# Trunk kernel on one Trainium2 core: the end of each layer of the second trunk with tokens in the partitions

## The reference

```
def trunk_layer(x, ctx, c, c_ctx, p, ang_r, ang_c, need_ctx):
    shift, scale, gate = jnp.split(jax.nn.silu(c) @ p['w_ada'] + p['b_ada'], 3, axis=-1)
    shift_c, scale_c, gate_c = jnp.split(jax.nn.silu(c_ctx) @ p['w_ada'] + p['b_ada'], 3, axis=-1)
    h = x * (1.0 + scale[:, None, :]) + shift[:, None, :]
    hc = ctx * (1.0 + scale_c) + shift_c
    ...                                   # 16 projections of h and hc, three branches
    out = merge(y_attn, y_gla, y_sgu, m_a, m_g, m_s)          # m @ p['w_out'] at its end
    x_new = layer_norm(DEEPNORM_ALPHA * x + gate[:, None, :] * out, p['post_g'], p['post_b'])
    if not need_ctx:
        return x_new, ctx                 # layer 1: only the 512 latent tokens
    ...
    ctx_new = layer_norm(DEEPNORM_ALPHA * ctx + gate_c * out_c, p['post_g'], p['post_b'])
    return x_new, ctx_new
```

## Time and profile before

| | us |
|---|---|
| median of 3 runs | 3522.41 (3520.08 to 3523.33) |
| the profiled execution | 3518.86 |
| its span in the trace | 3516.7 |
| PE busy in the span | 3188.0 |
| DVE busy | 1906.8 |
| ACT busy | 1178.4 |
| POOL busy | 208.4 |

### The profile page before, as it was taken

The page is one execution under the profiler, slowest core; times in us unless marked ns, Lnnn a source line. Parts: engine busy times, 40 slices in busy tenths (PEclk is TensorE's granted clock), DMA queues, the critical chain, the costliest instruction groups (busy, mean ns, idle before and its releaser), DMA issues.

```text
span 3516.7 us, 43743 instructions
## 1 busy us (share of the span) xinstructions
PE 3188.0 (91%) x18216; PEld 2645.0 (75%) x18216; DVE 1906.8 (54%) x2789; ACT 1178.4 (34%) x1763; POOL 208.4 (6%) x144
## 2 busy tenths in 40 slices
PE   7997889999988889999898999988998888997997
PEld 6886778888877667777777878756887777775776
DVE  7756555665434755777454443574434544457543
ACT  4234341221232544222342333253221534425322
POOL 0003100000010000000002120000001012100001
PEclk9999999999989999999899999999999799999997
DMA  5543123333211003555221123102113112320221
GB/s 203 178 154 126 55 78 126 121 131 120 84 55 60 1 13 121 179 176 177 88 86 69 65 75 110 42 1 81 54 66 96 71 66 88 103 81 7 97 94 58
DMA packets 91373, 321.84 MB, mean 92 GB/s; under 512 B 10070, under 2 KB 11991, under 8 KB 90025
## 3 DMA queue, kind: packets, MB, share of 16 engines
q1 hardware_dynamic: 81236, 289.43, 24.4%
q10 hardware_dynamic: 9940, 29.61, 2.3%
HBM read 297.26 MB, written 21.74 MB: 91 GB/s over the span
## 4 chain that ended last, share of the span: by engine, by line
PE 77%; DVE 10%; ACT 8%; issue 4%; DMA 1%; ACTq 0%; POOL 0%; SPq 0%; POOLq 0%; DVEq 0%
PE PS L384 76%; ACT whi L195 2%; ACT Pq L1274 1%; DVE STs L1311 1%; PE PS L387 1%; ACT nt L611 1%; DVE JUNK L514 1%; DVE stage L514 1%; DVE STq L1311 1%; DVE wlo L209 1%; ACT Ps L1274 1%; DMA Ht<-in_hT 1%; ACT U L616 0%; DVE fg L721 0%; ACT Ht L2304 0%
## 5 line engine op out<-in xcount | busy, mean ns | idle before, releaser
L384 PE MATMUL PS<-U,whi 128*128 128x512 f32 (+1 forms) x5408 | 1178.0, 363 | 93.7 <-DVE U L641 27.9
L384 PEld LDWEIGHTS PS<-U,whi 128*128 128x128 f32 x5408 | 913.8, 193 | 283.2 <-issue 59.3
L209 DVE TENSOR_TENSOR wlo<-stage,whi 128x1024 fp32r<-128x1024 f32 x339 | 417.0, 1232 | 1060.7 <-ACT whi L195 1060.1
L195 ACT ACTIVATE whi<-stage 128x1024 fp32r<-128x1024 f32 x339 | 358.3, 1058 | 1425.7 <-PE PS L384 1403.5
L384 PE MATMUL PS<-U,wlo 128*128 128x512 f32 (+1 forms) x2704 | 620.9, 355 | 0.0
L384 PE MATMUL PS<-Y,whi 128*128 128x512 f32 (+1 forms) x2240 | 582.9, 364 | 18.9 <-DVE Y L723 12.9
L384 PEld LDWEIGHTS PS<-U,wlo 128*128 128x128 f32 x2704 | 458.1, 189 | 79.7
L384 PEld LDWEIGHTS PS<-Y,whi 128*128 128x128 f32 x2240 | 397.3, 191 | 93.8 <-DVE Y L723 14.8
L384 PE MATMUL PS<-Y,wlo 128*128 128x512 f32 (+1 forms) x1120 | 367.7, 363 | 0.0
L384 PEld LDWEIGHTS PS<-Y,wlo 128*128 128x128 f32 x1120 | 208.9, 191 | 35.0
L384 PE MATMUL PS<-whi,U 128*128 128x512 f32 (+2 forms) x832 | 223.6, 359 | 11.3 <-DVE mV L1046 6.4
(11 more groups left out here) (412 smaller groups left out, 3279.3 us busy)
## 6 DMA issues: line engine op xcount, KB each, us to landing
stage<-in_w SPq DMA_DIRECT2D x128, 512.0 KB, 3.3
stage<-in_ada SPq DMA_DIRECT2D x80, 512.0 KB, 3.3
stage<-in_adb SPq DMA_DIRECT2D x48, 512.0 KB, 3.2
stage<-in_p_mg SPq DMA_DIRECT2D x16, 512.0 KB, 3.2
stage<-in_p_ma SPq DMA_DIRECT2D x16, 512.0 KB, 3.4
stage<-in_p_ms SPq DMA_DIRECT2D x16, 512.0 KB, 3.5
stage<-in_wo SPq DMA_DIRECT2D x16, 512.0 KB, 3.2
GS<-FS ACTq DMA_DIRECT2D x20, 384.0 KB
```

The lines of the kernel that those rows point to most:

```text
L195: act.activation(self.parts[r % n][0], self.stage[i % len(self.stage)], ACT.Copy).then_inc(*self.S.up("w_hi", i))
L209: dve.tensor_tensor(lo, self.stage[i % len(self.stage)], hi.bitcast(F32), ALU.subtract).then_inc(*self.S.up("w_lo", i))
L384: return pe.matmul(o, l, r, start=start, stop=stop_, skip_group_check=True)
```

## The change

The end of each layer is computed with the tokens in the partitions. `w_out` is cut into tiles of 256 rows by 512 columns. For the first 512 output features all token tiles (6 of 128 tokens in layer 0, 4 in layer 1) go through the four weight tiles one after the other. For the other 512 features each token tile goes through its four weight tiles in one go, and its residual and norm follow on DVE and ACT while PE has the next one. The gate is read as a row (`GR`), which goes out to DRAM as columns (`GROWS`) and comes back broadcast; the residual comes as rows (`XROWS`), gain and offset as rows (`PG`). In layer 0 each normed token tile is turned back by PE (`pe_turn_rows`), modulated by ACT and split for layer 1; POOL makes the rows of layer 1's residual. In layer 1 the normed rows are stored directly. For layer 0's residual PE turns four token tiles of `HT` into rows (`pe_turn_x`) at the start of the trunk. In layer 1 `p_gqk` 0 and 1 are computed for the 512 latent tokens only, and their two decay products come after both.

```diff
+        def pe_turn_x(pe, t):
+            s = B.take(pe, ("x", t), ("x_copy", t))
+            pe.wait_ge(*at("h_final", 7))
+            for k in range(8):
+                last = tr(pe, s[:, 128 * k:128 * k + 128], HT[:, k, 128 * t:128 * t + 128], 128)
+            last.then_inc(*up("x_turn", t))
+
+        def act_copy_x(act, t):
+            act.wait_ge(*at("x_turn", t))
+            act.activation(XT[t], B.of(("x", t)), ACT.Copy).then_inc(*up("x_copy", t))
...
+            if L:
+                s = B.take(pe, gate, ("g_af", L))
+                pe.wait_ge(*at("w_lo", gate))
+                pe.wait_ge(*at("u_lo", 1, 3))
+                pe_cols(pe, gate, s, xU, 0, LAT)
+                pe_turn_rows(pe, 5)
+                pe_proj(pe, q0, xU, False, ("g_qk", L, 0))
+                pe.wait_ge(*at("u_lo", 1, 5))
+                pe_cols(pe, gate, B.of(gate), xU, LAT, TOK).then_inc(*up("w_used", gate))
+                pe_proj(pe, T(f"p_gqk{L}", 1), xU, False, ("g_qk", L, 1))
+                decays(0)
+                decays(1)
+            else:
+                pe_proj(pe, gate, xU, True, ("g_af", L), xt=[("u_lo", L, k) for k in range(8)])
+                pe_turn_x(pe, 0)
+                pe_turn_x(pe, 1)
+                pe_proj(pe, q0, xU, True, ("g_qk", L, 0))
+                pe_turn_x(pe, 2)
+                pe_turn_x(pe, 3)
+                decays(0)
+                pe_proj(pe, T(f"p_gqk{L}", 1), xU, True, ("g_qk", L, 1))
+                decays(1)
...
         def pe_end(pe, L):
-            for k in range(8):
-                pe_proj(pe, T(f"wo{L}", k), xU, L == 0, ("e_g", L, k), xt=[("e_lo", L, k_) for k_ in range(8)] if k == 0 else None)
-            s = B.take(pe, ("e_mean", L), ("e_mean", L))
-            pe.wait_ge(*at("e_add", L, 7))
-            for a, b in cols(L == 0):
-                last = mm(pe, s[:, a:b], ONES, ACC[:, a:b], True, True)
-            last.then_inc(*up("e_sum", L))
-            pe_root(pe, 9 + 5 * L, [(LS[k], ("e_sq", L, k)) for k in range(8)], end_size(L) // 128, ("e_n", L, 7))
+            nt = token_tiles(L)
...
+            for u in range(4):
+                i = T(f"wo{L}", u)
+                pe.wait_ge(*at("w_lo", i))
+                pe.wait_ge(*at("e_lo", L, 2 * u + 1))
+                for t in range(nt):
+                    last = product(i, 0, t, u)
+                    if u == 3 and t < nt - 1:
+                        last.then_inc(*up("e_p", L, 0, t))
+                last.then_inc(*up("w_used", i))
+            for t in range(nt):
+                if t % 2 == 0:
+                    B.take(pe, ("e", L, 1, t // 2), ("e_m", L, 1, t + 1))
+                for u in range(4):
+                    i = T(f"wo{L}", 4 + u)
+                    if t == 0:
+                        pe.wait_ge(*at("w_lo", i))
+                    last = product(i, 1, t, u)
+                    if t == nt - 1:
+                        last.then_inc(*up("w_used", i))
+                if t < nt - 1:
+                    last.then_inc(*up("e_p", L, 1, t))
+                if L == 0 and t:
+                    pe_turn_rows(pe, t - 1)
...
+            act.wait_ge(*at("e_gain", 7))
+            for t in range(nt):
+                if t == nt - 1:
+                    W.hi(act, T("wo0", 5))
+                if t:
+                    modulate(t - 1, range(6))
+                root(t)
+                if t == nt - 2:
+                    W.hi(act, T("wo0", 4))
+                if t:
+                    modulate(t - 1, range(6, 8))
+                act.wait_ge(*at("e_nm", t))
+                act.activation(ROWS[:, t, :], ROWS[:, t, :], ACT.Identity, bias=EST[:, t, 15:16],
+                               scale=EST[:, t, 14:15]).then_inc(*up("e_x", t))
+                if t:
+                    upper(t - 1)
+            W.hi(act, T("wo0", 6))
+            modulate(nt - 1, range(8))
+            upper(nt - 1)
+            W.hi(act, T("wo0", 7))
...
+            def residual(h, t):
+                r = ROWS[:, t, half(h)]
+                dve.wait_ge(*at(*e_done(L, h, t)))
+                if h == 0 and t == 0:
+                    dve.wait_ge(*at("gr_in", L, 1))
+                dve.tensor_tensor(r, e_bank(L, h, t), GR[:, int(t >= 4), half(h)], ALU.mult).then_inc(*up("e_m", L, h, t))
+                dve.wait_ge(*at("e_m", L, h, t))
+                if h == 0:
+                    dve.wait_ge(*at(f"xr_in{t}", L))
+                dve.scalar_tensor_tensor(r, XR[:, t, half(h)], ALPHA, r, ALU.mult, ALU.add).then_inc(*up("e_r", L, h, t))
+                dve.wait_ge(*at("e_r", L, h, t))
+                dve.bn_stats(EST[:, t, 6 * h:6 * h + 6], r).then_inc(*up("e_bn", L, h, t))
...
+            for u in range(3):
+                dve_lo(dve, T(f"wo{L}", u))
+            for t in range(nt):
+                if t == nt - 1:
+                    dve_lo(dve, T(f"wo{L}", 3))
+                residual(0, t)
+            for t in range(nt):
+                if L == 0 and t == nt - 1:
+                    for u in range(4, 6):
+                        dve_lo(dve, T("wo0", u))
+                residual(1, t)
...
+                sp.wait_ge(*at("mod", T(f"adb{L}", 23), 1))
+                sp.dma_start(GROWS[L, :, :].rearrange("m p -> p m"), MODS[2 + L][:, 32:48],
+                             allow_slow_non_contiguous=True).then_inc(*dma("gr_out", L))
...
+                for v in range(2):
+                    sp.dma_start(GR[:, v, :].rearrange("q (k p) -> q k p", p=128),
+                                 GROWS[L, :, :].rearrange("(k v) p -> v k p", v=2)[v, :, :].partition_broadcast(128)).then_inc(
+                                     *dma("gr_in", L, v))
+                sp.wait_ge(*at("xs_out", L, 3))
+                for t in range(token_tiles(L)):
+                    rows = XROWS[128 * t:128 * t + 128, :] if t < 4 else A["ctx2R"][128 * t - 512:128 * t - 384, :]
+                    sp.dma_start(XR[:, t, :], rows).then_inc(*dma(f"xr_in{t}", L))
+                sp.dma_start(PG[:, :, :], A[f"post{L}"].partition_broadcast(128)).then_inc(*dma("pg_in", L))
+                W.load(sp, T(f"wo{L}", 7) + 1)
```

More of the change, by code:

```diff
@@ L1523, in pe_gla, with decays @@
             G = GL[L]
-            i = T(f"p_gate{L}", 0)
-            pe_proj(pe, i, xU, True, ("g_af", L), xt=[("u_lo", L, k) for k in range(8)])
-            for j in range(4):
-                pe_proj(pe, T(f"p_gqk{L}", j), xU, True, ("g_qk", L, j))
+            gate, q0 = T(f"p_gate{L}", 0), T(f"p_gqk{L}", 0)
+            def decays(j):
                 s = B.take(pe, ("g_z", L, j), ("g_b", L, j))
@@ new lines, in e_done, with e_bank, half, pe_turn_rows @@
+        def e_done(L, h, t):
+            return ("w_used", T(f"wo{L}", 4 * h + 3)) if t == token_tiles(L) - 1 else ("e_p", L, h, t)
+        def e_bank(L, h, t):
+            return B.of(("e", L, h, t // 2))[:, 512 * (t % 2):512 * (t % 2) + 512]
+        def half(h):
+            return slice(512 * h, 512 * h + 512)
+        def pe_turn_rows(pe, t):
+            s = B.take(pe, ("e_t", t), ("e_mod", t))
+            pe.wait_ge(*at("e_x", t))
+            for k in range(8):
+                last = tr(pe, s[:, 128 * k:128 * k + 128], ROWS[:, t, 128 * k:128 * k + 128], 128)
+            last.then_inc(*up("e_turn", t))
@@ new lines, in pe_end, with product @@
+        def pe_end(pe, L):
+            nt = token_tiles(L)
+            def product(i, h, t, u):
+                wh, wl = W.views(i, 2)
+                for kk in range(2):
+                    k = 2 * u + kk
+                    for q, (xr, wv) in enumerate(((0, wh), (1, wh), (0, wl))):
+                        last = mm(pe, e_bank(L, h, t), xU(xr, k, 128 * t, 128 * t + 128), wv[:, kk, :], k + q == 0,
+                                  k == 7 and q == 2)
+                return last
+            for j in range(nt // 2):
+                B.take(pe, ("e", L, 0, j), ("e_m", L, 0, 2 * j + 1))
+            for u in range(4):
[21 more added lines that the diff above has]
+                    pe_turn_rows(pe, t - 1)
@@ L2387, in pe_program @@
                 pe_end(pe, L)
-            pe.wait_ge(*at("l_out", 1, 7))
-            for i in range(4):
-                s = B.take(pe, ("out", i), ("o_copy", i))
-                for k in range(8):
-                    last = tr(pe, s[:, 128 * k:128 * k + 128], HT[:, k, 128 * i:128 * i + 128], 128)
-                last.then_inc(*up("o_turn", i))
         def act_program(act):
```

257 lines of the change are left out of this document (152 added, 105 removed).

## The result

The changed kernel takes 3457.75 us (median of 4 runs, 3455.53 to 3465.04), the kernel before in the same session 3521.24. The ratio is 0.9821, 95% interval 0.9809 to 0.9833: faster by 63.5 us, 1.8%. The forecast was 3455, in a range of 3444 to 3472, with a gain of 67.2.

A forecast was written before the change was run, and what follows sets the result against it. PE was taken as the bound, with gains at its idle or layout-only work around the layer ends. 39.5 + 32.7 - 5.0 = 67.2 off 3518.9 gives 3451.7; the runs' median lies 3.5 above, so 3455, range 3444 to 3472.

The forecast's parts named there:

- layer 0, to the start of `p_gv`: From layer 0's product with `w_out` to layer 1's `p_gv`, which would begin at 2774.8 instead of 2815.53: 40.7 gained.
- the clock in `p_gv`: Layer 1's `p_gv`: the 3.2 us wait before it may lower PE's clock; 1.2 us lost.
- layer 1's end: From layer 1's `w_out` product to the program's end, at 3484.0 instead of 3516.7: 32.7 us gained.
- turns of the input: Trunk's start: four turns of `HT`, 32 transposes in PE's full stream, cost 5.05 us.
- the work between: Stages between the changed parts, given no gain or loss of their own in the sum.
- signs of being wrong: DVE waits for `gr` or `xr`, ACT for the stage of `wo` 7 or `p_gv` 2, or PE for `rows` each cycle.
- The step that failed: POOL's rows for layer 1's residual, two 128x1024 steps a token tile: nobody waits before layer 1's `p_gv`; no cost.
- The first rival: Layer 0's second half: rows' chain exceeds PE's 6.9 us cycle if modulation takes over 0.56; 7.5 us, 3463, chance 12%.
- The turns of rows: Layer 0's second half: eight transposes per token tile on PE, 1.26 us each turn, six turns 7.6.
- the copy of `p_gqk`: Layer 1's start: PE waits 3.2 us before `p_gv` for ACT to copy `p_gqk` 3 out of PSUM.
- third rival: Gate rows take 36 us, or the gate's single-value store holds up `p_gv` 2 as much beyond slack: 3474, chance 6%.
- the slow rival: Both layer ends: gate rows' load takes above 64 us, making the kernel slower; at 70, 3542; chance 4%.

The follow-up runs named there:

- the decays' product early: Changed kernel with layer 1's first decay product moved ahead of the second query tile; 3461.91 us.
- run again: The changed kernel itself, unedited, measured a second time as the common measure; 3455.21 us, ratio 0.9811 of the kernel before.
- turns twice: Changed kernel with the eight transposes of each of the input's four turns made twice; 3454.77 us.
- rows not made: Changed kernel with POOL's gain and offset steps left out, so layer 1's residual is unscaled; 3450.88 us.
- rows on DVE: Changed kernel with POOL's gain and offset steps done by DVE, in its gap waiting for ACT; 3449.46 us, ratio 0.9796.
- quarters: Changed kernel with POOL's eight 128x1024 steps made as 32 of 128x256, at their old place; 3453.19 us.
- gate rows last: Changed kernel with the gate rows' loads put behind residual tiles, gains and `wo` 7 in SP's order; 3458.72 us.
- the rows late with the decays' product early: Changed kernel with POOL's rows after the third decay chain, stores one weight tile earlier, first decay product and its load early; 3450.7 us, ratio 0.9782.
- The two edits together: Changed kernel with gain and offset on DVE, plus the first decay product and its load early; 3458.74 us.
- the rows later: Changed kernel with POOL's rows made after layer 1's third decay chain, their stores after weight loads that `p_gv` needs; 3455.68 us.

## Why the prediction was right, and where a step of it was not

The time was forecast within 3 us, and the gain of 67.2 came out at 63.5. The mechanism of the two large terms holds: the one-column matmuls and hand-overs are gone, and the norm runs mostly under the products. By terms:

| term | forecast | measured |
|---|---|---|
| layer 0, to the start of `p_gv` | 40.7 | 32.7 |
| the clock in `p_gv` | -1.2 | -1.6 |
| layer 1's end | 32.7 | 33.6 |
| turns of the input | -5.0 | -3.5 |
| the work between | 0 | 2.0 |
| sum | 67.2 | 63.2 |

The 33.6 and 34.2 of the first table are reduced here by 0.9 and 0.6. The prediction had these for the blocks of `U` that the first weight tile needs, and they fall into PE's wait ahead of the first matmul (5.1 us instead of 4.2 in layer 0), in the stage before. So layer 0 is 8.0 us short, and the turns, layer 1 and the work between hide half of it: that the time came within 3 us is partly luck. Two of the prediction's own signs of being wrong came, without taking the time out of the range: PE waits for `rows` in each cycle, and ACT waits for a tile of `p_gv`.

- **The step that failed** is "POOL's rows, two 128x1024 steps a token tile, have nobody waiting before layer 1's `p_gv`". Nobody waits for the rows, but DVE's steps with both sources in SBUF wait while a POOL step runs, and with them the loop of DVE, ACT and PE. So the cycle was 8.55 and not 6.9. Without the rows the stage takes 126.8 us; the forecast for the same stretch was 127.4, or 126.5 without the 0.9 above. Both other ways of getting the rows out of DVE's way give 126.8 and 128.6. Their price is 7.8 to 9.3 us to `p_gv` in the two executions of the changed kernel, and 6.7 to 10.0 with the two kernels whose edit lies elsewhere. The five cycles alone are 7.7 longer; the rest of the spread comes from PE's last wait (see the waits) and the clock. That 126.8 is so near to the forecast is luck in part: without the rows the turns cost 2.6 less and the last wait 2.2 less than counted, and the clock some 3.4 that was not counted.
- **The first rival** had nearly this size (8.4 us a tile) and the wrong cause. It wanted a modulation over 0.56 us. Six of them take 2.21, so 0.37 each, and ACT's whole share is 5.6 us where 5.5 were counted; its step on the rows took 1.24, not 1.06. The chain that is too long goes through DVE. The prediction compared each engine's sum with PE's cycle. The loop through both engines is some 6.5 us even without POOL, so of the margin that it saw under 6.9 little was there.
- **The turns of rows** cost 6.47 - 5.64 = 0.83 each in the full stream, not 1.26; those of the input 3.5 in sum and not 5.05. Both prices came from a row behind an idle stretch, where the granted clock was 0.50 for the first part and 0.72 over the whole row. The 1.5 us on the input's turns are a mis-sized term, nothing more.
- **Waits.** `wo` 7 was waited for 1.2 us (1.5 forecast), the gate 2.0 (2.1), the copy of `p_gqk` before `p_gv` 2.5 and 4.1 in two executions (3.2). The described mechanism gives only some 1.0 of it: that is the wait in the runs where ACT waits little or not at all for a tile of `p_gv`, and with the decays' product early it is 0.6. The rest is a transfer. In the run again the chain before `p_gv` is this:

```profile
2757.22 14.35 DMA XROWS<-rows
2771.96 7.93 DMA stage<-in_p_gv
2779.91 1.06 ACT whi L198
```

  SP stands 12.4 us until the stores of the rows have landed, before it issues the last two tiles of `p_gv`, and ACT, which makes the decays' chain and the copy too, waits 3.2 for one of them. ACT's wait for that tile and PE's wait before `p_gv` go together: 0 and 0.9 (turns twice), 0.4 and 1.0 (rows not made), 1.2 and 2.5 (the profile after), 3.2 and 4.1 (run again), 3.3 and 2.7 (rows on DVE), 4.3 and 3.7 (quarters), 4.9 and 4.2 (gate rows last). The prediction had this in its third rival as a matter of the gate's store; no run here shows whether that store is what makes the rows' stores slow.
- **The clock.** 1.2 were allowed, for `p_gv` behind its wait. In the changed kernel the granted clock was at the lower level from 2720.6 to 2724.2, 1 us behind a wait of 1.9 and with PE busy throughout, and from 2737.6 to 2744.7, around a wait of 2.4 for the rows and one of 2.0 for the gate's weights, and `p_gv` took 35.4 instead of 33.85:

```profile
2741.00:2762.00 21.00, 21.00 (x100) 17.39 (x99) 10.22 (x13) 12.15 (x21) 0.00 (x0) 0.91 0.44 131
2788.00:2824.00 36.00, 35.42 (x146) 28.46 (x147) 19.35 (x19) 13.52 (x18) 4.37 (x4) 0.95 0.18 59
```

  Over 2720.5 to 2724.5 PE was busy for 4.00 us at 0.57, over 2737.5 to 2744.5 for 4.98 at 0.53: some 4 us ahead of `p_gv`, an estimate from these numbers, and 1.5 in it. Little of this is owed to the wait for the rows. In the run without POOL's rows two stretches of 4.1 us at 0.58 cost 3.4 in the same way, and `p_gv` took 35.4 as well, behind a wait of 1.0; in "turns twice" it took 33.85 behind one of 0.9, in the run again 36.4 behind one of 4.1.
- **Layer 1's end** was forecast at 55.5 us without the later start, and took 54.6: the product 46.8 (46.8), the chain on DVE 4.6 (5.2), the store and the end 3.2 (3.5).
- **Transfers** were rightly priced at nothing at the layers' ends, as "gate rows last" shows, and wrongly at layer 1's start, where the stores of the rows cost PE some 1.5 to 3.3 us (see the waits). The broadcast gate rows landed in 6.5 us, where X had to exceed 64 for the slow rival. The store of the gate as single values is the slow one:

```profile
gr<-GROWS SPq DMA_DIRECT2D x2, 512.0 KB, 6.5
...
GROWS<-MOD SPq DMA_DIRECT2D x1, 8.0 KB, 15.9
```

  8 KB took 15.9 us, more than twice what 512 KB of gate rows take. The Trainium skill ("DMA: Bandwidth & Descriptors", Specifications) puts the smallest transfer for the full rate at 512 B and has read-modify-write below it; the trace agrees that such a store is slow, and does not show why. With over 640 us until the rows are loaded back, nobody waited for it.

The Trainium skill ("SBUF — State Buffer", Terms, on the shared port pair) states the failed step's mechanism: VectorE and GpSimd share a pair of ports, and the one that has it holds it for its whole instruction. The trace agrees for the steps with two sources in SBUF (0.16 to 2.40, 0.69 to 2.17), and the run in quarters for "whole instruction". The prediction did not weigh it.

**What stays open.** Two versions look better than the changed kernel: the rows on DVE, and the rows late with the decays' product early. In the stage up to `p_mg` they gain 8.7 and 9.3 us over the run again; over "turns twice", whose stage is the shortest of the unchanged ones (170.4), it is 3.6 and 4.2. In whole times the second's interval, 0.9769 to 0.9796, ends below the run again's 0.9798 to 0.9825 by a hair, the first's overlaps it. So a gain in whole times is not shown for the first and barely for the second. The two edits together save 12.2 us up to `p_mg` and lose 11.4 between it and `w_out`, where the one piece costs 14.7 at the lower clock. What decides that fall was not tried; two kernels of three with the early product have it. Not tried either: the tiles of `p_gv` issued ahead of SP's wait for the rows' stores.

## What to carry to other kernels

- An engine that nobody waits for can still be waited for: before work is handed to POOL, look at which DVE steps with sources in SBUF will run beside it, and whether they stand in a loop with PE. A gap of DVE of the right length can be the cheaper place, even though DVE is then busier.
- Price an operation from a row at the clock and in the stream in which it will run. A row behind an idle stretch overstated the turns by 1.5 us of 5.
- Engines that wait for each other make a loop. Add up the loop from a step to the same step of the next tile, across the engines, and not each engine's share alone.
- A queue that waits for a store to land holds back the loads behind it, whoever needs them.
- Where effects are as large as the scatter of whole executions, cut each execution at the same instructions and compare stages. That also shows when a gain is lost in work that nobody touched.

## What the runs showed of the hardware

- The hold is by instruction and in both directions: DVE's 128x1 step took 2.40 us beside a POOL step of 2.40, and POOL's step 3.17 instead of 2.39 where DVE's split of `U` had begun first. It also caught steps with a single source in SBUF: TENSOR_SCALAR on 128x768 took 1.77 and 2.63 beside POOL in the run with the rows later, alone 0.56. The statistics (128x512, 0.69) and the product out of PSUM (0.68) were not held.
- The same 148 matmuls took 17.6 us at 2.4 GHz and 32.2 at 1.2 GHz, in kernels that differ only some 300 us earlier. With the rows on DVE and the early product the clock stayed at 0.50 while PE was busy for 20.00 of 20 us.
- Four stores of rows that were issued together landed in 7.0 to 9.9 us (median), in the run with later, single stores in 2.6.
- The untouched work from layer 0's `p_gv` to its `w_out` took 834.7 us in three kernels and about 838.5 in the others.
